# Two chained transformer blocks on one core: turning the first norm row into a column, and x as it lands

## What is computed

```python
def rms_norm(x, g):
    y = xf * lax.rsqrt(jnp.mean(xf * xf, axis=-1, keepdims=True) + NORM_EPS)
    return (y * g.astype(jnp.float32)).astype(x.dtype)

def moba_attention(xn, w_qkv, w_o, cos, sin):
    qkv = (xn @ w_qkv).reshape(b, s, 3, N_HEADS, HEAD_DIM)
```

## Time and profile before

| | us |
|---|---|
| median of 3 runs | 1089.14 (1088.73 to 1089.78) |
| span of the profiled execution, first to last instruction | 1086.7 |
| PE busy (matmuls) | 1073.5 (99%) |
| DVE busy | 740.5 (68%) |
| ACT busy | 560.8 (52%) |
| POOL busy | 40.2 (4%) |

### The profile page before, as it was taken

The page is one execution under the profiler, slowest core; times in us unless marked ns, Lnnn a source line. Parts: engine busy times, 40 slices in busy tenths (PEclk is TensorE's granted clock), DMA queues, the critical chain, the costliest instruction groups (busy, mean ns, idle before and its releaser), DMA issues.

```text
span 1086.7 us, 15287 instructions
## 1 busy us (share of the span) xinstructions
PE 1073.5 (99%) x5810; PEld 908.4 (84%) x5810; DVE 740.5 (68%) x1044; ACT 560.8 (52%) x723; POOL 40.2 (4%) x59
## 2 busy tenths in 40 slices
PE   8999999999999999999999999999999999999997
PEld 6888888888888888888878888888889778888886
DVE  5756665656686656568877975665897878666665
ACT  5556444435455444346665544445653766444453
POOL 1000000000000000000000220000300300000000
PEclk9999999999999999999999999999999999999999
DMA  9953366564547564637532755657576324754651
GB/s 332 338 168 116 92 218 212 155 217 169 171 148 236 179 207 158 228 106 204 176 110 78 237 191 195 193 165 255 156 237 228 92 79 156 232 185 163 206 180 39
DMA packets 127162, 195.83 MB, mean 180 GB/s; under 512 B 6977, under 2 KB 97217, under 8 KB 126994
## 3 DMA queue, kind: packets, MB, share of 16 engines
q1 hardware_dynamic: 123904, 185.77, 51.8%
q0 software_dynamic: 3216, 9.51, 3.0%
q10 hardware_dynamic: 2, 0.00, 0.0%
HBM read 194.21 MB, written 1.05 MB: 180 GB/s over the span
## 4 chain that ended last, share of the span: by engine, by line
PE 95%; DVE 3%; ACT 1%; issue 1%; DVEq 0%; DMA 0%; ACTq 0%
PE ps L2099 25%; PE ps L2000 15%; PE ps L2002 15%; PE ps L2001 15%; PE ps L2102 13%; PE ps L2181 2%; PE ps L2220 1%; PE ps L2042 1%; PE ps L2597 1%; PE ps L2183 1%; DVE act L1237 1%; PE ps L2246 1%; PE ps L2595 1%; PE ps L2632 1%; PE ps L2279 1%
## 5 line engine op out<-in xcount | busy, mean ns | idle before, releaser
L2099 PE MATMUL ps<-act,whi 128*128 128x512 f32 x1200 | 424.4, 397 | 0.0
L1112 DVE TENSOR_TENSOR wlo<-raw,whi 128x2048 fp32r<-128x2048 f32 (+2 forms) x161 | 363.9, 2277 | 87.5 <-ACT whi L672 87.1
L2102 PE MATMUL ps<-act,wlo 128*128 128x256 f32 x1200 | 336.7, 281 | 0.0
L672 ACT ACTIVATE whi<-raw 128x2048 fp32r<-128x2048 f32 (+2 forms) x170 | 317.6, 1887 | 26.7 <-PE ps L2002 20.6
L2099 PEld LDWEIGHTS ps<-act,whi 128*128 128x128 f32 x1200 | 225.2, 188 | 53.7
L2102 PEld LDWEIGHTS ps<-act,wlo 128*128 128x128 f32 x1200 | 226.7, 189 | 2.0
L2002 PE MATMUL ps<-whi,hlo 128*128 128x512 f32 x400 | 157.1, 393 | 0.0
L2000 PE MATMUL ps<-whi,hhi 128*128 128x512 f32 x400 | 156.7, 392 | 0.1
L2001 PE MATMUL ps<-wlo,hhi 128*128 128x512 f32 x400 | 156.6, 392 | 0.0
L2000 PE MATMUL ps<-whi,act 128*128 128x512 f32 (+2 forms) x286 | 112.4, 393 | 1.5 <-DVE act L1812 0.6
L2002 PE MATMUL ps<-whi,act 128*128 128x512 f32 (+2 forms) x286 | 108.0, 378 | 0.0
(11 more groups left out here) (230 smaller groups left out, 1154.5 us busy)
## 6 DMA issues: line engine op xcount, KB each, us to landing
raw<-mlp_w_up_in SPq DMA_DIRECT2D x32, 1024.0 KB, 6.5
raw<-mlp_w_down_in SPq DMA_DIRECT2D x32, 1024.0 KB, 4.9
raw<-ffn_w_gate_in SPq DMA_DIRECT2D x22, 1024.0 KB, 5.4
raw<-ffn_w_up_in SPq DMA_DIRECT2D x22, 1024.0 KB, 5.3
raw<-ffn_w_down_in SPq DMA_DIRECT2D x22, 1024.0 KB, 4.9
raw<-attn_w_qkv_in SPq DMA_DIRECT2D x10, 1024.0 KB, 9.2
raw<-w_kv_shared_in SPq DMA_DIRECT2D x8, 1024.0 KB, 5.3
raw<-attn_w_o_in SPq DMA_DIRECT2D x4, 1024.0 KB, 5.0
```

Of the source, the lines that this page charges most:

```text
L672: nc.scalar.activation(whi[:, s, 0:width], raw[:, s, 0:width], ACT.Copy).then_inc(hi_ready, 1)
L1112: nc.vector.tensor_tensor(wlo[:, s, 0:width], raw[:, s, 0:width], whi[:, s, 0:width].bitcast(F32), ALU.subtract).then_inc(lo_ready, 1)
L2099: nc.tensor.matmul(bank(b + f), lhsT=w[0][:, at:at + P], rhs=act[:, k, :, :].rearrange("p a t -> p (a t)"), start=k == 0, stop=False, skip ...
L2102: ins = nc.tensor.matmul(bank(b + f, 0, T), lhsT=w[1][:, at:at + P], rhs=act_hi[:, k, :], start=False, stop=k == KT - 1, skip_group_check= ...
```

## The change

The norm row is no longer spread over the partitions. PE turns it, 128 channels at a time, into a column for each block k (`turn_first_row`), and DVE copies the 8 columns into `first_gain`. x is turned as loaded (`turn_x`), with no multiply before it. The multiply by the row now happens in the split of the turned quarter, per partition, as the channels lie there: ACT writes the high part as bank times column (`first_hi`), and DVE the low part as bank times column minus high part (`first_lo`). As the column differs for each k, a quarter takes four instructions of 128 columns instead of one of 512, on both engines. The quarters go half by half instead of tile by tile: 0 is half 0 of tile 0, 1 half 0 of tile 1, 2 half 1 of tile 0, 3 half 1 of tile 1. They are turned in the order 0, 2, 1, 3. Six identity matmuls stand ahead of quarter 0 and four ahead of quarter 1. The order on ACT and DVE is written anew. POOL issues the loads of the positions once chunk 1 has landed.

```diff
-        BY_TILES = ("mix0", "mlp0", "mix1", "mlp1", "fpre0", "kvsrc", "fpre1")
+        BY_TILES = ("mlp0", "mix1", "mlp1", "fpre0", "kvsrc", "fpre1")
...
+            pool.wait_ge(w_loaded[SLOT[1]], 16)
             for n, name in enumerate(("positions", "positions_2")):
...
-            copy_turned("mix0", (0,))
+            def first_hi(p, count):
+                h, t, _ = quarter("mix0", p)
+                act.wait_ge(turned, count)
+                for k in range(4 * h, 4 * h + 4):
+                    ins = nc.scalar.activation(act_hi[:, k, t * P:(t + 1) * P],
+                                               bank(4 + p, (k % 4) * P, (k % 4 + 1) * P), ACT.Copy,
+                                               scale=first_gain[:, k:k + 1])
+                ins.then_inc(act_hi_ready, 1)
+
+            act.wait_ge(first_gain_copied, 1)
+            first_hi(0, 1)
             hi_part_of(0, 0, first_half_loaded, first_half_hi)
-            copy_turned("mix0", (1, 2))
+            first_hi(1, 3)
             hi_part_of(0, 1, w_loaded[SLOT[0]], hi_ready)
+            first_hi(2, 3)
             hi_part_of(1, 0, second_half_loaded, second_half_hi)
-            copy_turned("mix0", (3,))
+            first_hi(3, 4)
             hi_part_of(1, 1, w_loaded[SLOT[1]], hi_ready)
...
-            def first_gained(p):
-                h, t, cols = quarter("mix0", p)
-                nc.vector.tensor_tensor(xs[:, t, cols], x[:, t, cols], bank(2 + h), ALU.mult).then_inc(xs_ready, 1)
+            def first_lo(p):
+                h, t, _ = quarter("mix0", p)
+                dve.wait_ge(act_hi_ready, p + 1)
+                for k in range(4 * h, 4 * h + 4):
+                    at = act_hi[:, k, t * P:(t + 1) * P]
+                    ins = nc.vector.scalar_tensor_tensor(out=act_lo[:, k, t * P:(t + 1) * P],
+                                                         in0=bank(4 + p, (k % 4) * P, (k % 4 + 1) * P),
+                                                         scalar=first_gain[:, k:k + 1], in1=at.bitcast(F32),
+                                                         op0=ALU.mult, op1=ALU.subtract)
+                ins.then_inc(act_lo_ready, 1)
...
-            dve.wait_ge(first_row_spread, 1)
+            dve.wait_ge(first_row_turned, 1)
+            nc.vector.tensor_copy(first_gain[:, :], bank(2, 0, KT)).then_inc(first_gain_copied, 1)
+            release_row()
             dve.wait_ge(x_loaded, 16)
             dve.sem_inc(x_ready, 2)
-            first_gained(0)
-            first_gained(1)
-            split_turned("mix0", (0,))
+            dve.wait_ge(first_gain_copied, 1)
+            first_lo(0)
+            lo_part_of(0, 0, first_half_hi, 1, first_half_lo)
             dve.wait_ge(x_rest_loaded, 16)
             dve.sem_inc(x_ready, 2)
-            first_gained(2)
-            lo_part_of(0, 0, first_half_hi, 1, first_half_lo)
-            split_turned("mix0", (1,))
-            first_gained(3)
-            split_turned("mix0", (2,))
+            first_lo(1)
             lo_part_of(0, 1, hi_ready, 1, lo_ready)
-            dve.wait_ge(xs_ready, 4 * XSR["mix0"] + 4)
-            release_row()
+            first_lo(2)
             lo_part_of(1, 0, second_half_hi, 1, second_half_lo)
-            split_turned("mix0", (3,))
+            first_lo(3)
             lo_part_of(1, 1, hi_ready, 2, lo_ready)
+            dve.sem_inc(xs_ready, 4)
...
+            def turn_first_row():
+                pe.wait_ge(ones_made, 1)
+                pe.wait_ge(first_row_loaded, 16)
+                for k in range(KT):
+                    ins = nc.tensor.transpose(bank(2, k, k + 1), rows[0:1, 0, k * P:(k + 1) * P], scale_row[0:1, 0:1])
+                ins.then_inc(first_row_turned, 1)
+
+            def turn_x(p):
+                h, t, _ = quarter("mix0", p)
+                pe.wait_ge(*((x_rest_loaded, 16) if t else (x_loaded, 16)))
+                for k in range(4 * h, 4 * h + 4):
+                    ins = nc.tensor.transpose(bank(4 + p, (k % 4) * P, (k % 4 + 1) * P),
+                                              x[:, t, k * P:(k + 1) * P], ident)
+                ins.then_inc(turned, 1)
...
-            turn("mix0", parts=(0, 1, 2))
+            turn_first_row()
+            pe.wait_ge(const_loaded, 16)
+            for _ in range(6):
+                nc.tensor.matmul(bank(3, 0, P), lhsT=ident, rhs=ident, start=True, stop=True)
+            turn_x(0)
+            turn_x(2)
+            for _ in range(4):
+                nc.tensor.matmul(bank(3, 0, P), lhsT=ident, rhs=ident, start=True, stop=True)
+            turn_x(1)
...
-                                wait_acts("mix0", c + 1 + 2 * t)
+                                wait_acts("mix0", 2 * c + t + 1)
...
-                                turn("mix0", parts=(3,))
+                                turn_x(3)
```

More of the change, by code:

```diff
@@ L189, in two_blocks @@
         soft = sb("soft", [P, 4, 2 * (8 + 8 + 16)])
+        first_gain = sb("first_gain", [P, KT])
         qk_tok = arena[:, 0:4096].rearrange("p (t n) -> p t n", t=TT)
@@ L242, in two_blocks @@
         ones_made = sem("ones_made")
-        first_row_spread = sem("first_row_spread")
+        first_row_turned = sem("first_row_turned")
+        first_gain_copied = sem("first_gain_copied")
         const_loaded = sem("const_loaded")
@@ L2022, in turn @@
             def turn(name, blocks=((0, 4), (4, 8)), parts=range(4)):
[L2024 to L2031, removed]
                 for p in parts:
                     h, t, _ = quarter(name, p)
-                    if name == "mix0":
-                        for _ in range((3, 0, 3, 0)[p]):
-                            nc.tensor.matmul(bank(7, 0, P), lhsT=ident, rhs=ident, start=True, stop=True)
                     if name in BUSY:
```

## The result

The changed kernel takes 1092.05 us (median of 22 runs, 1089.58 to 1093.96), the kernel before beside it 1089.68 (22 runs, 1088.73 to 1091.65). The ratio is 1.0019, with the interval 1.0013 to 1.0025: slower by some 2 us, where 0.5 us faster was forecast and the range ended at 1089.9. In the experiments further down seven runs, one of them of the kernel before, took 1171 to 2726 us, and both the ratios and the medians leave them out.

The account below looks back on a forecast made before the run. PE, busy 99% of the span, bounds the kernel, so only the entry could pay: head start 1.0 us, capped before chunk 4 at 0.24 + 0.25 = 0.5, so 1089.14 - 0.5 = 1088.6 us; range 1087.7 to 1089.9.

Parts of the forecast that it names:

- ACT starts at 7.15: Entry: ACT starts right after PE's turn 0, forecast to end at 7.1; 1.3 us earlier than before.
- rival B: Entry: PE still at 1.2 GHz in the first tile's products; head start gone, 1089.1 (to 1089.5); chance 0.08.
- Row transposes: Entry on PE: eight one-column transposes at 0.15 us each replace the row matmuls, ending at 3.5 (2.3 to 4.0).
- Six identities and turn 0: Entry on PE: identities take 2.7 us, to 6.2 (5.0 to 7.2), then turn 0 takes 0.87, to 7.1.
- Groups of four: Split of a turned quarter: four instructions cost 1.2 us on ACT and on DVE; upper bounds 1.5 and 1.4.
- the head start: PE at the second tile's products: starts 12.1 to 12.7 against 13.38, so 0.7 to 1.3 us earlier, 1.0 taken.
- The gate's two terms: Before chunk 4: PE's gain is capped by 0.24 us cover plus 0.25 from an earlier copy out of banks 0 and 1.
- The 1.7 us are paid again: Moved position loads: their 1.7 us transfer shortfall recurs at some 15 to 17 us, still ahead of chunk 3.
- rival A: Head start carries through: chunk 3 lands with its full 1.7 us; gain 0.8 to 1.0, about 1088.2; chance 0.20.
- C: Position loads land late at 26.9, DVE's angles start 1.1 to 1.3 late; net +0.9 to +1.1, 1090.2; chance 0.10.
- D: Entry: transposes and split instructions cost upper bounds, identities bind; first product 11.9, net 0, 1089.1; chance 0.08.
- the bank copy caps the gain: Before chunk 4: the copy out of banks 0 and 1 caps the gain at 1.0 us; faster by more 0.04.

Follow-up runs that it names:

- The early table: The changed kernel plus a one-element ACT activation ahead of the waits, so that ACT's table load runs early: 1088.83 us, ratio 0.9997.
- where the squares were moved: The changed kernel with table early, turn 3 behind turn 1, squares ahead of ACT's chunk 3, sine and cosine ahead of the root: 1087.47 us, ratio 0.9984.
- the one kept busy: The changed kernel plus twelve identity matmuls on PE behind its third turn (turn 1), table load still late: 1090.35 us, ratio 1.0007.
- the second profile of the changed kernel: The changed kernel measured again with nothing altered, in the rounds of other experiments: 1091.2 us, ratio 1.0014.
- the run with the positions behind chunk 3: The changed kernel with table early, turn 3 behind turn 1, and position loads waiting for chunk 3 instead of chunk 1: 1090.43 us, ratio 1.0015.

## Why the prediction was wrong, step by step

**The step that failed: "ACT starts at 7.15".** The sum has no term for the table load. It ended at 2.59 in the kernel before, long before anyone needed ACT, and I took it as fixed there. The change adds a wait ahead of ACT's first activation, and I didn't ask what is queued behind it there. Price: 1.28 us, on the chain in full (8.54 against 7.15; the first product at 12.11 against 10.7). The early table undoes exactly this, and the added wait in the kernel before brings it about.

**The second: PE's idle time.** I priced the clock only as rival B, as a clock that rises late, and against it I said that the identities and turns are dense and start sooner. They are, and PE's pace had doubled by 8.85. The sign of being wrong that I named, matmuls after 13 us that change their pace, is there: 0.43 apart up to 18.5 us, 0.23 behind it. But by my own sum PE had nothing to do from about 9.3, turn 1's end, to 10.7, and I didn't read what such a gap does. With the table load it became 2.7 us and cost up to 2.9. So B's effect came by another way than B's. The Trainium skill's rule that I set beside B, on transposes and the clock, wasn't what decided: the clock was high once the turns and identities had run, and fell where PE did nothing. No run tells the share of the transposes in its rise.

**What was right.** Row transposes end at 3.45 (3.5). Six identities and turn 0 end at 7.18 (7.1). Groups of four take 1.14 and 1.13 us (1.2). With the table early, the first product is at 10.83 (10.7), the head start 1.20 (1.0), and the net 0.69 (0.5), with a 0.51 stall ahead of chunk 4 released by the copy out of the banks, in that experiment as in the changed kernel. The forecast time (1088.6) is that of this kernel (1088.83), not of the one it was made for, and that it comes so close is in part luck, as the next point shows.

**The gate's two terms were both off, and made up for each other.** The copy moved by 0.71 us (34.17 to 32.72 + 0.74 = 33.46), not by 0.25, as ACT had chunk 3 without waiting for it. The cover of 0.24 was no cover: PE's product follows that copy by 0.15 at its closest (33.46 to 33.61), and then restarts more slowly. Together some 0.7 + 0 instead of 0.25 + 0.24, of a head start of 1.20.

**"The 1.7 us are paid again" was mis-sized.** It is 0.54 us in the new place. Chunk 3 landed 13.2 after its issue, at 18.1, where I had 19.0. In this rival A was right: most of the dip belongs to the place at the start. Its carry-through came only where the squares were moved.

**C** didn't occur: positions issued at 12.86 landed 4.5 later, at 17.4, 0.7 before chunk 3, which had been issued 8 us ahead of them. Issued at 18.6 they took 6.7 and were late.
That they overtook chunk 3 is what the Trainium skill's page DMA: Bandwidth & Descriptors, SWDGE vs HWDGE vs iDMA, has by its turns between queues; by its rule C gives no loss, and here it gave none. **D** didn't occur either: the first product at 12.11 is near its 11.9, but by the table load, and the groups of four cost 1.14 and 1.13 instead of 1.5 and 1.4. (Its sum also took 2.9 for the identities, where their upper bound was 3.2.)

**The chances.** I gave 0.07 to slower and let the range end at 1089.9, on the ground that the bank copy caps the gain. It caps the gain only. Nothing in the trace capped the loss. No case had ACT's table load in it, and the one with the clock, B, ended at 1089.5.

**What stays open.** Why the clock stays down for 3.4 us in one profile and 6.8 in another, in which share of the runs it falls at all (the mean clocks suggest at least half), and why it held behind one gap of 2.2 us and fell behind another of 2.3. Where PE loses 0.8 us between 614 and 757 us in the first profile of the changed kernel and 1.8 behind 614 us in that of the one kept busy, when the second profile of the changed kernel shows 0.2 there. And what the place of the positions is worth in the changed kernel itself.

## What to carry to other kernels

Before a wait is put ahead of an engine's first instruction, look for what the engine does before it on its own, such as a table load, and give that something to run on early: one element is enough. Then list the gaps that the new order leaves on TensorE ahead of dense work, since a gap costs its length and, where the clock falls, as behind those of 2.3 and 2.7 us here, the products behind it at half pace; if it can't be closed, put matmuls in it, as the run with PE kept busy did. And where an entry is made faster, ask which copy or buffer the gain meets 20 us later, and move that first.

## What the runs showed of the hardware

Where this kernel's first activation needs one semaphore, the table load ahead of it is free (it starts at 1.31); with a wait for two the load itself waits for the later one (8.60, and 6.89 to 7.32 in four profiles of the changed kernel and its variants). The load takes 1.28 us. The granted clock fell to 1.2 GHz behind 2.67 and 2.27 us without a matmul, and stayed there for some 6.8 and 3.4 us, with PE in full work from 12.11 and 11.89 on. It stayed at 2.4 GHz behind 1.32 us, behind 1.37 and 1.59 us with a turn between, and also behind 2.23 us ahead of chunk 4, in the run with the positions behind chunk 3. Two loads of 256 numbers each by the software queue cost 1.7 us of transfer when issued at 1.3 us, and 0.54 when issued at 12.9 (0.3 to 0.9 in other profiles with that place). A transpose of one column takes 0.12 us (0.98 for eight), next to 0.22 for one of 128, both ahead of the doubling of the pace.
